# A hybrid decoder block on one core: product operands at the low end of SBUF, a new order for the first loads and casts, halved first units of the norms, and two users of ScalarE's tables swapped

## The chip, the cores and the metric

The kernel runs on one core of one Trainium2 chip, as one launch. The metric is the device time of that launch in microseconds. Weights and activations are float32 in HBM; the kernel streams some 503 MB of them through the core once.

## The reference

One decoder layer for 256 tokens of width 2048: a half-step SwiGLU feed-forward, a token mixer with eight dilated-attention heads and eight retention heads in parallel, a second half-step feed-forward, and a final RMSNorm. Each sub-layer reads a normed and modulated input; shifts, scales and gates come from one conditioning vector `c`.

```python
ada = (silu(c) @ w_ada + b_ada).reshape(9, D)          # shift, scale, gate, three times
h = rmsnorm(x, g_ffn1) * (1 + sc1) + sh1
x = x + 0.5 * gt1 * ((silu(h @ w1_gate) * (h @ w1_up)) @ w1_down)     # 2048 -> 5632 -> 2048
h = rmsnorm(x, g_mix) * (1 + sc2) + sh2
proj = h @ w_in                                        # 2048 -> 6144, split into q, k, v of both kinds and a gate
y = concat(dilated_attention(aq, ak, av), retention(rq, rk, rv) * silu(rg))
x = x + gt2 * (y @ w_out)                              # 2048 -> 2048
h = rmsnorm(x, g_ffn2) * (1 + sc3) + sh3
x = x + 0.5 * gt3 * ((silu(h @ w2_gate) * (h @ w2_up)) @ w2_down)
out = rmsnorm(x, g_final)
```

## The kernel before

Every large product is done in three passes of the reduced format fp32r. A factor is split into a rounded part and the rest ("hi" and "lo"), and `product_chunk` adds hi·hi, hi·lo and lo·hi in one PSUM bank. The activations are the stationary operand (128x128, loaded by LDWEIGHTS) and the weights the moving one (128x512).

- **Chunks.** All weights lie in HBM as 656 chunks of 128x1024 float32 (512 KB), in the order in which they are used. A chunk goes through a ring of four slots: SyncE loads it into `w_raw`, ScalarE writes its rounded part into `w_hi` (`w_hi`, L613), VectorE the rest into `w_lo` (`w_lo`, L808), and TensorE takes it with 12 matmuls (2 tiles of the contraction, 2 halves of the tokens, 3 passes; L1069, L1070, L1071). At the two inner norms, two chunks more are prepared in `w_hi_ahead` and `w_lo_ahead`.
- **Stationary operands.** There are three: `x_split` (the normed input, hi and lo), `hidden` (silu(gate) times up, hi and lo) and `projections_split` (the mixer's output, hi and lo). `hidden`, `projections`, `ada_early` and `x_turned` share one region of 48 KB per partition.
- **Groups.** A `Group` is the run of chunks that fills two PSUM banks. Feed-forward groups are GATE, UP and DOWN, those of the mixer IN and OUT. Their order is written out by `plan()`. GATE, UP and IN read `x_split`; DOWN reads `hidden`; OUT reads `projections_split`.
- **Order of the rest.** `schedule()` puts every other stage behind a chunk number: TensorE does its part of a stage after that chunk, and ScalarE and VectorE do theirs between the casts of the chunks. Each engine walks the table in its own program, and semaphores join them.
- **The opening.** `opening()` is the order of the first 68 chunks, in which the columns of `w_ada` are multiplied on VectorE too (`ada_tile`, L820, 1 MB each, four buffers `ada_early`). `x` is normed by ScalarE in quarters of 512 columns (`normed_first`, L671), turned by TensorE (`turn_x`, L1112, all eight ahead of the first product in TensorE's program), copied out of PSUM (`keep_x`, L676), and modulated slice by slice as soon as its columns of `w_ada` are done (`modulate_first`, L685 and L689; `low_first`, L932). Slice i of `x_split` is waited for by `operand`.
- **The inner norms** (`boundary(n, res)`). The last four chunks of a DOWN or OUT group are done for one half of the tokens and then for the other (`tail`). While the second half is multiplied, the first is normed. A norm is cut into eight units of 128 tokens by 512 columns (`UNITS`): `normed` (L926), `turn_unit` (L1123), `modulate` (L698), `split_x` (L941, L942). `head` does the first four chunks of the next group for one half and then the other, with the turning of later units between them.
- **The heads.** Square roots (`std`, L734) and SiLU (`silu_g`, L739) need different activation tables on ScalarE; a load of a table is an instruction of its own. `gated` (L1022), `turn_y` (L1201) and `split_ret` (L743, L1027) bring the retention output, in four pairs p of heads, into `projections_split`.

The lines that place the shared region and the ahead tiles are these:

```python
top = (nc.sbuf_usable_end - HID_BYTES) // 512 * 512
late_at = top - LATE * D * 4
hid = nc.alloc_sbuf_tensor_at("hidden", [P, FA * NT, 2 * T], F32R, offset=top)
proj_r = nc.alloc_sbuf_tensor_at("projections_split", [P, MIX_IN // P, T], F32R, offset=top)
```

In the built program this gives the following byte addresses within a partition (first byte to the byte behind the last), before and in the changed kernel:

```
tile                          before               changed
x_split (stationary)           32896 to  65664      65664 to  98432
w_hi (moving)                  82048 to  98432      98432 to 114816
w_lo (moving)                  98432 to 114816     114816 to 131200
scratch0 to scratch3          114816 to 131200     163968 to 180352
table (with the identity)     131200 to 145032     180352 to 194184
w_hi_ahead, w_lo_ahead        163328 to 179712     212480 to 228864
hidden, projections_split     179712 to 228864      16512 to  65664
residual, w_raw                16512 and 65664     131200 and 147584
```

Of the kernel before, what the change touches and what calls it, by code (L numbers as in the profile page):

```python
# [6 lines left out]
F32 = mybir.dt.float32  # L7
# [6 lines left out]
P = 128  # L14
# [90 lines left out]
UNITS = ((0, 0), (0, 1), (1, 0), (1, 1), (0, 2), (1, 2), (0, 3), (1, 3))  # L105
# [27 lines left out]
def schedule():  # L133
# [6 lines left out]
    def boundary(n, res):  # L140
# [7 lines left out]
        def units(name, *numbers):  # L148
            return [(name, 8 * n + u) for u in numbers]

        if n == 3:
# [6 lines left out]
        put(c0 + 4, *units("split_x", 2, 3), *units("xn", 4, 5, 6, 7), *units("mod", 4, 5))  # L158
        put(c0 + 5, *units("split_x", 4, 5), *units("mod", 6))
        put(c0 + 6, *units("split_x", 6), *units("mod", 7))  # L160
        put(c0 + 7, *units("split_x", 7))
# [54 lines left out]
    put(RET_FROM + 17, ("silu_g", 0), ("std", 1))  # L216
# [35 lines left out]
def opening():  # L252

    order = [("ada", i) for i in range(4)] + [("scale", 0), ("w", 0), ("low", 0)]
# [56 lines left out]
def build(nc, x_in, c_in, w_ada, b_ada, gains_in, g_final, w_all, table_in_hbm, out_t):  # L311
    with ExitStack() as ctx:  # L312
# [39 lines left out]
        HID_BYTES = FA * NT * 2 * T * 4  # L352
        assert HID_BYTES == (MIX_IN // P) * T * 4 == EARLY * D * 4 + DT * T * 4
        top = (nc.sbuf_usable_end - HID_BYTES) // 512 * 512
        late_at = top - LATE * D * 4
# [4 lines left out]
        hid = nc.alloc_sbuf_tensor_at("hidden", [P, FA * NT, 2 * T], F32R, offset=top)  # L360
        proj = nc.alloc_sbuf_tensor_at("projections", [P, MIX_IN // P, T], F32, offset=top)
        proj_r = nc.alloc_sbuf_tensor_at("projections_split", [P, MIX_IN // P, T], F32R, offset=top)
        ada_early = nc.alloc_sbuf_tensor_at("ada_early", [P, EARLY, D], F32, offset=top)
# [999 lines left out]
```

## Time and profile before

| | |
|---|---|
| median of 3 runs | 1925.22 us (1924.96 to 1925.38) |
| the profiled execution | 1925.92 us, its span 1924.1 us |
| TensorE matmul busy | 1882.3 us, 98% of the span |
| TensorE weight load busy | 1545.5 us, 80% |
| VectorE busy | 1310.5 us, 68% |
| ScalarE busy | 850.9 us, 44% |
| HBM read | 503.10 MB, 263 GB/s over the span |

The span runs from the first to the last instruction that the profiler saw. The 1.8 us between it and the time of the execution lie around the program. Busy shares are averages over stages with different limits.

### The profile page before, as it was taken

Reading aid. Unit: us, or ns where it says so; the run is one execution under the profiler, and the core shown is the slowest. Engines: PE = TensorE matmul, PEld = TensorE weight load, DVE = VectorE, ACT = ScalarE, POOL = GpSimd, SP = SyncE. Lnnn points to the kernel's source line nnn. Section 1 sums busy time; section 2 is a strip of 40 time slices with the busy share of each in tenths; the row PEclk is TensorE's granted clock in tenths of the full one; section 3 lists DMA queues with packets and bytes.
Section 4 is the critical chain, followed back from the end, with each engine's and each line's share of the span. In section 5 each row is a group of like instructions: output and inputs, shape, how many; then the busy total and the mean of one; then the engine's idle time right before and its main releaser. Section 6 shows DMA issues by size and latency. Waiting matters only on the chain. (4 is left out here: it accounts for less than half of the span.)

```text
span 1924.1 us, 21150 instructions
## 1 busy us (share of the span) xinstructions
PE 1882.3 (98%) x8392; PEld 1545.5 (80%) x8392; DVE 1310.5 (68%) x1350; ACT 850.9 (44%) x969; POOL 0.2 (0%) x4
## 2 busy tenths in 40 slices
PE   5899999999999999999999999999999999999998
PEld 4688888888888888788887787888888888888886
DVE  7798987887878878776665677666655454444454
ACT  5444444334444444645543546444443334444443
POOL 0000000000000000000000000000000000000000
PEclk7899999999999999999999999999999999999999
DMA  9898899888888887696454565777765556556563
GB/s 391 346 403 343 323 366 357 339 324 342 345 334 335 331 330 292 217 337 243 154 165 143 185 243 172 285 281 280 258 210 185 191 182 200 188 191 209 188 191 133
DMA packets 117889, 506.61 MB, mean 263 GB/s; under 512 B 13728, under 2 KB 13984, under 8 KB 98464
## 3 DMA queue, kind: packets, MB, share of 16 engines
q1 hardware_dynamic: 117792, 505.27, 72.0%
q8 instruction: 66, 1.08, 0.2%
q14 instruction: 31, 0.25, 0.0%
HBM read 503.10 MB, written 2.12 MB: 263 GB/s over the span
## 5 line engine op out<-in xcount | busy, mean ns | idle before, releaser
L808 DVE TENSOR_TENSOR w_lo<-w_raw,w_hi 128x1024 fp32r<-128x1024 f32 x652 | 795.1, 1223 | 516.0 <-ACT w_hi L613 515.4
L613 ACT CAST w_hi<-w_raw 128x1024 fp32r<-128x1024 f32 x652 | 684.1, 1051 | 1005.4 <-PE banks L1071 957.4
L1069 PE MATMUL banks<-w_hi,x_split 128*128 128x512 f32 x1776 | 703.2, 396 | 16.2 <-DVE x_split L932 16.2
L1071 PE MATMUL banks<-w_hi,x_split 128*128 128x512 f32 x1776 | 695.3, 391 | 0.0
L1070 PE MATMUL banks<-w_lo,x_split 128*128 128x512 f32 x1776 | 694.4, 391 | 0.0
L1069 PEld LDWEIGHTS banks<-w_hi,x_split 128*128 128x128 f32 x1776 | 335.7, 189 | 86.0 <-issue 13.2
L1071 PEld LDWEIGHTS banks<-w_hi,x_split 128*128 128x128 f32 x1776 | 335.2, 189 | 71.3
L1070 PEld LDWEIGHTS banks<-w_lo,x_split 128*128 128x128 f32 x1776 | 335.8, 189 | 68.1
L1069 PE MATMUL banks<-w_hi,hidden 128*128 128x512 f32 x704 | 278.2, 395 | 0.0
L1071 PE MATMUL banks<-w_hi,hidden 128*128 128x512 f32 x704 | 277.8, 395 | 0.0
L1070 PE MATMUL banks<-w_lo,hidden 128*128 128x512 f32 x704 | 277.7, 395 | 0.0
L820 DVE CUSTOM_DVE_ANT_0 scratch<-ada_raw,cond_row,ada 128x2048 bf16<-128x2048 f32 x112 | 262.7, 2345 | 0.1
L1071 PEld LDWEIGHTS banks<-w_hi,hidden 128*128 128x128 f32 x704 | 132.6, 188 | 30.9
L1070 PEld LDWEIGHTS banks<-w_lo,hidden 128*128 128x128 f32 x704 | 132.7, 188 | 30.8
L1069 PEld LDWEIGHTS banks<-w_hi,hidden 128*128 128x128 f32 x704 | 132.6, 188 | 30.7
L820 DVE CUSTOM_DVE_ANT_0 scratch<-ada_early,cond_row,ada 128x2048 bf16<-128x2048 f32 x32 | 75.1, 2347 | 1.4 <-DVE ada L820 0.6
L1069 PE MATMUL banks<-w_hi,projections_split 128*128 128x512 f32 x128 | 50.8, 397 | 0.0
L1071 PE MATMUL banks<-w_hi,projections_split 128*128 128x512 f32 x128 | 50.5, 395 | 0.0
L1070 PE MATMUL banks<-w_lo,projections_split 128*128 128x512 f32 x128 | 50.5, 394 | 0.0
L1071 PEld LDWEIGHTS banks<-w_hi,projections_split 128*128 128x128 f32 x128 | 24.1, 188 | 5.6
L1069 PEld LDWEIGHTS banks<-w_hi,projections_split 128*128 128x128 f32 x128 | 24.1, 188 | 5.5
L1070 PEld LDWEIGHTS banks<-w_lo,projections_split 128*128 128x128 f32 x128 | 24.1, 189 | 5.5
(133 smaller groups left out, 603.5 us busy)
## 6 DMA issues: line engine op xcount, KB each, us to landing
w_raw<-w_chunks SPq DMA_DIRECT2D x656, 512.0 KB, 4.2
ada_raw<-w_ada_tiles SPq DMA_DIRECT2D x112, 1024.0 KB, 6.0
ada_early<-w_ada_tiles SPq DMA_DIRECT2D x32, 1024.0 KB, 9.3
gate_row<-gate_rows SPq DMA_DIRECT2D x3, 1024.0 KB, 7.0
residual<-x_t SPq DMA_DIRECT2D x2, 1024.0 KB, 5.9
out_t<-residual SPq DMA_DIRECT2D x4, 512.0 KB, 3.1
table<-tables SPq DMA_DIRECT2D x1, 1664.0 KB, 9.7
cond_row<-g_final_t SPq DMA_DIRECT2D x1, 1024.0 KB, 5.4
```

Source lines behind the costliest of these rows:

```text
L613: nc.scalar.copy(w_parts(c)[0], raw[:, c % RING, :]).then_inc(hi_ready, 1)
L808: nc.vector.tensor_tensor(lo, raw[:, c % RING, :], hi.bitcast(F32), ALU.subtract).then_inc(lo_ready, 1)
L820: nc.vector.tensor_tensor_reduce(junk, src, c_row[:, :], 1.0, ada[:, m:m + 1], ALU.mult, ALU.add, ada[:, m:m + 1]).then_inc(ada_step, 1)
L1069: nc.tensor.matmul(o, x_hi, hi, start=(first and k == k0), stop=False, skip_group_check=True)
L1070: nc.tensor.matmul(o, x_hi, lo, start=False, stop=False, skip_group_check=True)
L1071: ins = nc.tensor.matmul(o, x_lo, hi, start=False, stop=(last and k == k0 + KC - 1), skip_group_check=True)
```

## The change

Four things change.

1. **Addresses.** The shared region (`hidden`, `projections_split` and what shares it) goes from the top of SBUF to the bottom, under the new name `stationary`; `x_split`, `w_hi` and `w_lo` follow it, and `residual` and `w_raw` come behind them. The ahead tiles go to the very top. No instruction of a product changes but for its addresses.
2. **The opening.** The first tile of `w_ada` is loaded ahead of `x`, the second between the halves of `x`. Both sums of squares are taken by ScalarE (the one on VectorE goes), and each engine copies one half of `cond_row` out of PSUM. VectorE does two tiles of `w_ada` before the reciprocal of the root. ScalarE does the cast of chunk 0 and the first modulation before the third quarter of `normed_first`, and the casts of chunks 1 and 2 move among the rest.
3. **Units of the norms.** The first two quarters of each half are cut in a unit of 2+2 tiles and one of 4; a norm has ten units now.
4. **The heads.** `std` 1 comes ahead of `silu_g` 0; `turn_y` and `split_ret` of pairs 2 and 3 come one chunk later.

```diff
-UNITS = ((0, 0), (0, 1), (1, 0), (1, 1), (0, 2), (1, 2), (0, 3), (1, 3))
+QUARTERS = ((0, 0), (0, 1), (1, 0), (1, 1), (0, 2), (1, 2), (0, 3), (1, 3))
+UNITS = ((0, 0, 2), (0, 2, 2), (0, 4, 4), (1, 0, 2), (1, 2, 2), (1, 4, 4), (0, 8, 4), (1, 8, 4), (0, 12, 4), (1, 12, 4))
...
-        put(c0 + 2, sums[0][0], sums[0][3], *units("xn", 0, 1), *units("mod", 0, 1))
-        put(c0 + 3, *units("split_x", 0), sums[1][0], *units("split_x", 1), *sums[1][1:], *units("xn", 2, 3),
-            *units("mod", 2, 3))
+        put(c0 + 2, sums[0][0], sums[0][3], *units("xn", 0, 1), *units("mod", 0, 1, 2))
+        put(c0 + 3, *units("split_x", 0, 1), sums[1][0], *units("split_x", 2), *sums[1][1:], *units("xn", 2, 3),
+            *units("mod", 3, 4, 5))
...
-    put(RET_FROM + 17, ("silu_g", 0), ("std", 1))
+    put(RET_FROM + 17, ("std", 1), ("silu_g", 0))
...
-        put(RET_FROM + 25 + p - 1, ("turn_y", p))
-        put(RET_FROM + 25 + p - 1, ("split_ret", p))
+        put(RET_FROM + 25 + p, ("turn_y", p))
+        put(RET_FROM + 25 + p, ("split_ret", p))
...
-    order = [("ada", i) for i in range(4)] + [("scale", 0), ("w", 0), ("low", 0)]
+    order = [("ada", 0), ("ada", 1), ("inverse", 0), ("ada", 2), ("ada", 3), ("scale", 0), ("w", 0), ("low", 0)]
...
-        xs = sb("residual", [P, 2, D])
+        low = (nc.sbuf_base + 31) // 32 * 32
+        sb("stationary", [P, HID_BYTES // 4])
         xsp = sb("x_split", [P, DT, 2 * T], F32R)
-        raw = sb("w_raw", [P, RING, CH])
         whi = sb("w_hi", [P, RING, CH], F32R)
         wlo = sb("w_lo", [P, RING, CH], F32R)
+        xs = sb("residual", [P, 2, D])
+        raw = sb("w_raw", [P, RING, CH])
...
-        top = (nc.sbuf_usable_end - HID_BYTES) // 512 * 512
-        late_at = top - LATE * D * 4
+        late_at = (nc.sbuf_usable_end - LATE * D * 4) // 512 * 512
...
-        hid = nc.alloc_sbuf_tensor_at("hidden", [P, FA * NT, 2 * T], F32R, offset=top)
+        hid = nc.alloc_sbuf_tensor_at("hidden", [P, FA * NT, 2 * T], F32R, offset=low)
...
+        def unit_count(m):
+
+            return SLICES + NU * (m[0] - 1) + m[1] + 1
...
+        def last_before(n, u):
+
+            quarter = QUARTERS.index((UNITS[u][0], UNITS[u][1] // 4)) - 2
+            if quarter < 0:
+                return SLICES + NU * (n - 1)
+            return SLICES + NU * (n - 1) + max(i for i, (t, k, _) in enumerate(UNITS) if QUARTERS.index((t, k // 4)) == quarter) + 1
...
             sp.dma_start(tab[:, 0:EARLY_COLS], table_in_hbm[:, 0:EARLY_COLS]).then_inc(ident_in, 16)
-            sp.dma_start(xs[:, 0, :], x_in[:, 0, :]).then_inc(x_in_sem[0], 16)
+            early_tile(0)
             sp.dma_start(ada[:, :], b_ada).then_inc(const_in, 16)
             sp.dma_start(gain[:, :, :], gains_in).then_inc(const_in, 16)
+            sp.dma_start(xs[:, 0, :], x_in[:, 0, :]).then_inc(x_in_sem[0], 16)
+            early_tile(1)
             sp.dma_start(xs[:, 1, :], x_in[:, 1, :]).then_inc(x_in_sem[1], 16)
-            for i in range(EARLY):
+            for i in range(2, EARLY):
                 early_tile(i)
...
             keep_x(0)
             keep_x(1)
+            w_hi(0)
+            modulate_first(0)
             normed_first(2)
             keep_x(2)
             keep_x(3)
+            w_hi(1)
             normed_first(3)
-            w_hi(0)
-            modulate_first(0)
             keep_x(4)
             keep_x(5)
-            w_hi(1)
+            w_hi(2)
             keep_x(6)
             keep_x(7)
-            w_hi(2)
             w_hi(3)
...
                     for i in range(TAIL):
                         if t == 0:
                             pe.wait_ge(lo_ready, g.first + i + 1)
-                            if i >= 2:
-                                turn_unit(8 * n + i)
+                            if i == 2:
+                                turn_unit(n, 3)
+                                turn_unit(n, 4)
+                            elif i == 3:
+                                turn_unit(n, 5)
```

**ScalarE in the opening, before.** The rows from the first root on; `scratch<-residual` is `normed_first`, `x_turned<-banks` is `keep_x`, `w_hi<-w_raw` a cast of a chunk.

```order
L671 ACTIVATE scratch<-residual,inverse_root 128x512 x4
L676 COPY x_turned<-banks 128x512 x2
L671 ACTIVATE scratch<-residual,inverse_root 128x512 x2
L676 COPY x_turned<-banks 128x512 x2
L671 ACTIVATE scratch<-residual,inverse_root 128x512 x2
L613 CAST w_hi<-w_raw 128x1024
L685 ACTIVATE scratch<-x_turned,ada,mod_scale 128x256 x2
L689 CAST x_split<-scratch 128x2x256
L676 COPY x_turned<-banks 128x512 x2
L613 CAST w_hi<-w_raw 128x1024
```

The same place in the changed kernel:

```order
L693 ACTIVATE scratch<-residual,inverse_root 128x512 x4
L698 COPY x_turned<-banks 128x512 x2
L635 CAST w_hi<-w_raw 128x1024
L707 ACTIVATE scratch<-x_turned,ada,mod_scale 128x256 x2
L711 CAST x_split<-scratch 128x2x256
L693 ACTIVATE scratch<-residual,inverse_root 128x512 x2
L698 COPY x_turned<-banks 128x512 x2
L635 CAST w_hi<-w_raw 128x1024
L693 ACTIVATE scratch<-residual,inverse_root 128x512 x2
L698 COPY x_turned<-banks 128x512 x2
L635 CAST w_hi<-w_raw 128x1024
```

The cast of chunk 0 and the first modulation moved ahead of the last two quarters of `normed_first`; behind the modulation, the cast of chunk 1 now has a quarter and two copies ahead of it where it had two copies.

**VectorE at the first inner norm, before.** From the split of the first unit on; `banks,gate_row` and `residual<-residual,scratch` are the residual of the second half of the tokens.

```order
L941 CAST x_split<-scratch 128x4x128
L942 TENSOR_TENSOR x_split<-scratch,x_split 128x4x128
L885 TENSOR_TENSOR scratch<-banks,gate_row 128x512
L891 TENSOR_TENSOR residual<-residual,scratch 128x512
L941 CAST x_split<-scratch 128x4x128
L942 TENSOR_TENSOR x_split<-scratch,x_split 128x4x128
L901 RECIPROCAL inverse_root<-root 128x1
```

The same place in the changed kernel:

```order
L965 CAST x_split<-scratch 128x2x128
L966 TENSOR_TENSOR x_split<-scratch,x_split 128x2x128
L965 CAST x_split<-scratch 128x2x128
L966 TENSOR_TENSOR x_split<-scratch,x_split 128x2x128
L908 TENSOR_TENSOR scratch<-banks,gate_row 128x512
L914 TENSOR_TENSOR residual<-residual,scratch 128x512
L965 CAST x_split<-scratch 128x4x128
L966 TENSOR_TENSOR x_split<-scratch,x_split 128x4x128
L924 RECIPROCAL inverse_root<-root 128x1
```

The first split is done in two halves; the residual of the second half of the tokens still stands between it and the next quarter's split.

**ScalarE in the heads, before.** `projections<-projections` is `silu_g`, `var<-var` is `std`, `projections_split<-banks` is `split_ret`.

```order
L739 ACT_TABLE_LOAD
L739 ACTIVATE projections<-projections 128x1024
L734 ACT_TABLE_LOAD
L734 ACTIVATE var<-var 128x8
L613 CAST w_hi<-w_raw 128x1024 x3
L743 CAST projections_split<-banks 128x512
L613 CAST w_hi<-w_raw 128x1024
L743 CAST projections_split<-banks 128x512
L613 CAST w_hi<-w_raw 128x1024 x3
L638 COPY projections<-banks 128x4x128 x2
L613 CAST w_hi<-w_raw 128x1024
L739 ACT_TABLE_LOAD
```

The same place in the changed kernel, up to the second `silu_g`:

```order
L757 ACTIVATE var<-var 128x8
L762 ACT_TABLE_LOAD
L762 ACTIVATE projections<-projections 128x1024
L635 CAST w_hi<-w_raw 128x1024 x3
L766 CAST projections_split<-banks 128x512
L635 CAST w_hi<-w_raw 128x1024
L766 CAST projections_split<-banks 128x512
L635 CAST w_hi<-w_raw 128x1024 x3
L660 COPY projections<-banks 128x4x128 x2
L635 CAST w_hi<-w_raw 128x1024
L762 ACTIVATE projections<-projections 128x1024
L635 CAST w_hi<-w_raw 128x1024 x2
```

Two of the three table loads are gone, the one ahead of the second `silu_g` among them, and one more cast of a chunk stands between that `silu_g` and the next `split_ret`.

## Rows read from the trace of the kernel before

**Rows 1.** The page, busy time, share of the span and instructions of TensorE.

```profile
PE 1882.3 (98%) x8392; PEld 1545.5 (80%) x8392; DVE 1310.5 (68%) x1350; ACT 850.9 (44%) x969; POOL 0.2 (0%) x4
```

**Rows 2.** Waits of TensorE: who waited for whom, us, times, longest.

```profile
PE banks L1069 <- DVE x_split L932: 16.2, 4, 5.1
PE banks L1112 <- ACT scratch L671: 8.4, 3, 6.9
PE banks L1069 <- DVE x_split L942: 2.2, 2, 1.1
PE banks L1201 <- DVE projections L1022: 1.6, 1, 1.6
PE banks L1123 <- DVE scratch L926: 1.2, 4, 0.5
```

**Rows 3.** Windows, TensorE alone: stretch, busy (count), clock, DMA.

```profile
100.00:200.00 100.00, 100.00 (x443) 1.00 0.94 368
340.00:440.00 100.00, 100.00 (x432) 1.00 0.87 335
1110.00:1160.00 50.00, 50.00 (x217) 1.00 0.65 230
```

**Rows 4.** The page's groups: one pass of each stationary operand.

```profile
L1069 PE MATMUL banks<-w_hi,x_split 128*128 128x512 f32 x1776 | 703.2, 396 | 16.2 <-DVE x_split L932 16.2
...
L1069 PE MATMUL banks<-w_hi,hidden 128*128 128x512 f32 x704 | 278.2, 395 | 0.0
...
L1069 PE MATMUL banks<-w_hi,projections_split 128*128 128x512 f32 x128 | 50.8, 397 | 0.0
```

**Rows 5.** Timeline, first norm: first and last of ten steps on ahead tiles.

```profile
783.19 0.39 PE L1070 MATMUL banks<-w_lo_ahead,x_split 128*128 128x512 f32 x1
...
785.51 0.40 PE L1071 MATMUL banks<-w_hi_ahead,x_split 128*128 128x512 f32 x1
```

**Rows 6.** Timeline of the opening: start us, us, instruction, idle before.

```profile
16.63 1.33 ACT L671 ACTIVATE scratch<-residual,inverse_root 128x512 f32<-128x512 f32 x2
20.21 1.09 PE L1112 MATMUL banks<-table,scratch 128*128 128x128 f32 x8 [1.10 <-ACT scratch L671]
24.51 1.06 ACT L676 COPY x_turned<-banks 128x512 f32<-128x512 f32 x2
25.47 1.06 ACT L613 CAST w_hi<-w_raw 128x1024 fp32r<-128x1024 f32 x1
25.48 0.77 PE L1069 MATMUL banks<-w_hi,x_split 128*128 128x512 f32 x1 [4.18 <-DVE x_split L932]
26.56 1.23 DVE L808 TENSOR_TENSOR w_lo<-w_raw,w_hi 128x1024 fp32r<-128x1024 f32 x1 [1.22 <-ACT w_hi L613]
38.79 0.39 PE L1071 MATMUL banks<-w_hi,x_split 128*128 128x512 f32 x1
44.31 0.77 PE L1069 MATMUL banks<-w_hi,x_split 128*128 128x512 f32 x1 [5.13 <-DVE x_split L932]
76.00 0.69 DVE L932 TENSOR_TENSOR x_split<-scratch,x_split 128x512 fp32r<-128x512 f32 x1 [0.72 <-ACT x_split L689]
```

**Rows 7.** Timeline of the first inner norm.

```profile
780.05 2.90 ACT L698 ACTIVATE scratch<-banks,ada,mod_scale 128x128 f32<-128x128 f32 x8 [1.17 <-issue]
782.80 1.09 ACT L613 CAST w_hi<-w_raw 128x1024 fp32r<-128x1024 f32 x1
782.88 0.47 PE L1069 MATMUL banks<-w_hi_ahead,x_split 128*128 128x512 f32 x1 [1.09 <-DVE x_split L942]
784.10 0.64 ACT L654 ACTIVATE scratch<-residual 128x512 f32<-128x512 f32 x1 [0.21 <-DVE residual L891]
```

**Rows 8.** Timeline of the heads, around the third `turn_y`.

```profile
1087.63 1.28 ACT L739 ACT_TABLE_LOAD   x1
1088.92 1.06 ACT L739 ACTIVATE projections<-projections 128x1024 f32<-128x1024 f32 x1
...
1090.83 0.66 PE L1201 MATMUL banks<-table,projections 128*128 128x128 f32 x4 [1.56 <-DVE projections L1022]
```

More of the change, by code:

```diff
@@ L148, in units @@
         def units(name, *numbers):
-            return [(name, 8 * n + u) for u in numbers]
+            return [(name, (n, u)) for u in numbers]
         if n == 3:
@@ L691, in modulate @@
             def modulate(m):
-                n, t, q, u = unit(m)
+                n, u = m
+                t, k0, tiles = UNITS[u]
                 act.wait_ge(scl_ready, SLICES + n)
-                act.wait_ge(xt_done, m + 1)
-                act.wait_ge(mod_ready, m - 1)
-                for i in range(4):
-                    k = 4 * q + i
-                    ins = nc.scalar.activation(plain(u)[:, i * P:i * P + P], ps[:, 4 + u % 4, i * P:i * P + P], ACT.Identity,
+                act.wait_ge(xt_done, unit_count((n, max(i for i, (half, k, _) in enumerate(UNITS) if (half, k // 4) == (t, k0 // 4)))))
+                act.wait_ge(mod_ready, last_before(n, u))
+                for i in range(tiles):
+                    k = k0 + i
+                    ins = nc.scalar.activation(plain_unit(u)[:, i * P:i * P + P], turned(u)[:, i * P:i * P + P], ACT.Identity,
                                                scale=scl[:, k:k + 1], bias=ada[:, 3 * n * DT + k:3 * n * DT + k + 1])
@@ L922, in normed @@
             def normed(m):
-                n, t, q, u = unit(m)
+                n, (t, q) = m[0], QUARTERS[m[1]]
                 if q >= 2:
-                    dve.wait_ge(xt_done, 8 * n + UNITS.index((t, q - 2)) + 1)
+                    last = max(u for u, (half, k, _) in enumerate(UNITS) if half == t and k // 4 == q - 2)
+                    dve.wait_ge(xt_done, unit_count((n, last)))
                 nc.vector.tensor_scalar(xn_buf(t, q), xs[:, t, GW * q:GW * q + GW], rinv[:, t:t + 1], None,
@@ L1114, in turn_x, with turn_unit @@
                 ins.then_inc(xt_done, 1)
-            def turn_unit(m):
-                n, t, q, u = unit(m)
-                pe.wait_ge(xn_ready, xn_count(m))
-                if u >= 4:
-                    pe.wait_ge(mod_f32, m - 3)
-                x = xn_buf(t, q)
-                for i in range(4):
-                    ins = nc.tensor.transpose(ps[:, 4 + u % 4, i * P:i * P + P], x[:, i * P:i * P + P], ident)
+            def turn_unit(n, u):
+                t, k, tiles = UNITS[u]
+                quarter = QUARTERS.index((t, k // 4))
+                pe.wait_ge(xn_ready, xn_count(n, t, k // 4))
+                if quarter >= 4:
+                    pe.wait_ge(mod_f32, SLICES + NU * (n - 1) + FREED[quarter])
+                x = xn_buf(t, k // 4)
+                for i in range(tiles):
+                    at = (k % 4 + i) * P
+                    ins = nc.tensor.transpose(turned(u)[:, i * P:i * P + P], x[:, at:at + P], ident)
                 ins.then_inc(xt_done, 1)
@@ L1245, in tail @@
                         if t == 1 and i == g.count - 1 and n < 3:
-                            turn_unit(8 * n)
-                            turn_unit(8 * n + 1)
+                            for u in range(3):
+                                turn_unit(n, u)
                         ins = product_chunk(g.first + i, halves(hid) if g.kind == DOWN else mixed, KC * i, 2 * g.side, False,
@@ L1289, in _ @@
                     if start and i % 2 == 0:
-                        pe.wait_ge(mod_ready, 8 * norm + min(i + 2, 8))
+                        pe.wait_ge(mod_ready, unit_count((norm, 7 if i == TAIL else NU - 1)))
                     chunk(g, i)
```

87 lines of the change are left out of this document (47 added, 40 removed).

## The prediction

> **What bounds the kernel now.** I read the page first: TensorE is busy for 98% of the span [rows 1], so only what lets a matmul follow the last one sooner, or takes a gap of TensorE away, can shorten the kernel. Then the waits of TensorE. They add up to some 30 us [rows 2], nearly all in the first 80 us: 16.2 us in four waits for a slice of `x_split`, 8.4 us for the normed `x`. Behind the opening TensorE waits twice for the first unit of an inner norm (2.2 us), four times for a later unit (1.2 us), and once in the heads, for `gated` (1.6 us). Everything else is matmul after matmul.
>
> So the question becomes what one matmul costs, and the busy time doesn't tell it: matmuls overlap, and their mean duration is 395 to 397 ns for all three stationary operands [rows 4]. What counts is the step from start to start. The windows give it. A matmul of 0.39 us is counted if it touches the window, so the step is (window + 0.39) / count. Between 100 and 200 us all products read `x_split`: 100.39 / 443 = 226.6 ns. Between 340 and 440 us all read `hidden`: 100.39 / 432 = 232.4 ns. Between 1110 and 1160 us all read `projections_split`: 50.39 / 217 = 232.2 ns [rows 3]. The granted clock is 1.00 in all three (the 2.4 GHz level), and the instructions have the same form. TensorE had no wait in the two slower stretches, and VectorE, ScalarE and the DMA engines are no busier there (DMA 0.94, 0.87, 0.65). What differs is where the stationary operand lies: 32,896 to 65,664 in the first, 179,712 and up in the other two.
>
> A second row speaks for the address and against the tile: at the first inner norm `x_split`, at its low place, is multiplied by the ahead tiles at 163,328 to 179,712. Ten steps take 785.51 - 783.19 = 2.32 us, 232 ns each [rows 5]. Either operand at a high address costs the same some 5.7 ns. Within the low region I see no slope: the 226.6 ns is a mean over `x_split` from 32,896 to 65,664 and over weights from 82,048 to 114,816. So it looks like a line between 114,816 and 163,328.
>
> **The addresses.** `hidden` is read by 3 x 704 matmuls and `projections_split` by 3 x 128 [rows 4], 2496 together. Each goes from 232.35 to 226.65 ns: 2496 x 5.7 = 14.2 us off. All of it lies on TensorE, which nothing else covers, so it comes off the end. The ahead tiles stay high; their 48 matmuls gain nothing. The cost side: `w_lo` now lies at 114,816 to 131,200, where no product operand has lain, and `x_split` as the stationary operand at 65,664 to 98,432, where so far only moving operands lay. The bounds are 0 (as all rows below 114,816) and 5.7 ns for each of the 3 x 1776 = 5328 matmuls of `x_split`, 30.4 us. I take 0: the new places are nearer to the region that is fast than to the nearest one known slow (163,328). The turning of tiles reads the identity and the scratch tiles, which go higher; eight turnings take 1.09 us [rows 6], and as the identity lies above 131,200 before as after, I take 0 there too.
>
> At this point a page speaks against the change. The Trainium skill, "TensorE: Matmul & The Clock Gate", section "Wait — 56ns, not 53.3ns?", gives start to start as the columns over the clock and some 2.5 ns, about 216 ns for 512 columns, and knows no address in it. By that rule the first term would be nothing. The trace differs from it in both stretches, with 226.6 and 232.4 ns.
>
> **The opening.** TensorE turns all of `x` before its first product. Before, the last eight turnings started at 20.21 and the first product at 25.48, when slice 0 was split [rows 6]. That split keeps its time: it needs the same 2 MB of `x` and 4 MB of `w_ada` to arrive, whatever their order. But now two quarters of `normed_first` stand behind it. From the end of the first modulation, 24.5: a quarter 1.33, two copies 1.06, a cast 1.06, a quarter 1.33, less some 0.1 of overlap at each, ends near 28.9; eight turnings of 1.09 us bring the first product to 30.1, 4.6 us later. This is covered: the first four chunks ended at 39.0 (last matmul at 38.79 [rows 6]) and TensorE then waited 5.1 us for slice 1, until 44.31. They end at 43.6 now. What is late instead is VectorE. Its `w_lo` of chunk 1 had waited 1.22 us for the cast at 25.47 and started at 26.56; the cast has a quarter more ahead of it, so it starts near 27.8, 1.2 us later. Behind it stand in one queue the tiles of `w_ada` and rests of chunks up to the split of slice 3 at 76.00 [rows 6], with next to no idle time, and TensorE waits for each slice at 44.31 and twice more. From there it never waits until the first norm. So +1.2 us reach the end. Bounds: 0, if the small gaps of VectorE absorb it, and +3, if the late first product holds back casts (they wait for its chunks) or TensorE's clock rises later after its last gap. The new order of the loads costs and gives nothing: the same bytes stand ahead of the fourth tile of `w_ada`, and the earlier first two `ada_tile` end in a wait for it.
>
> **The norms.** The first unit's modulation of eight tiles starts at 780.05 and takes 2.90 us, 0.36 a tile [rows 7]. With two tiles to wait for and a half-size split (half of 1.15 us and a fixed part, 0.75), the first half unit is ready at 780.05 + 0.75 + 0.75 = 781.6, just as TensorE ends the tail. The first wait, 1.1 us before 782.88, nearly goes. But `head` puts the turning of the second half's units ahead of its third chunk, and these come from the residual of the second half, whose sum of squares started at 784.10, behind ScalarE's cast that ended at 783.89 [rows 7]. That cast stays, so the second half is ready 0.15 us sooner at most. TensorE runs two chunks 1.1 us sooner and waits 1.1 us longer there. I take 0.15 us off at each of two norms, 0.3 in all; bounds 2.2 off (both waits really gone) and 0.6 on (extra fixed costs on VectorE).
>
> **The heads.** `turn_y` of pair 2 waited for `gated`, that for the SiLU at 1088.92, and that for the table load of 1.28 us at 1087.63 [rows 8]. The load goes, since nothing between the two SiLUs asks for another table, and TensorE comes a chunk (2.8 us) later. The last matmul ahead started at 1088.87 (1090.83 less the wait and a step), so the gap of 1.7 us beyond a normal step closes. OUT needs pairs 2 and 3 at its seventh and eighth chunk, three chunks after the turning, against some 2 us of ScalarE and VectorE work. `std` ahead of `silu_g` 0 puts 0.2 us on the first `gated`, which TensorE doesn't wait for. I take 1.7 off, bounds 1.3 and 1.9.
>
> **The sum.** -14.2 - 1.7 - 0.3 + 1.2 = -15.0 us. The profiled execution took 1925.92 us, 0.7 above the median of the runs, so it goes to 1910.9 and the median of 1925.22 to **1910.2 us**. Its own bounds: 1906 (opening 0, norms 2.2, heads 1.9) to 1913 (opening 3, norms 0.6 on, heads 1.3: 1925.2 - 11.9).
>
> **The rivals.** A change of 0.2% (3.9 us) is about what this measurement can tell from none.
>
> - **The line lies lower (slower).** If it is crossed by the new `w_lo` or, for stationary operands, by the new `x_split`, the 5328 matmuls of `x_split` slow down. With `hidden` still gaining, 1910.2 + 30.4 = 1940.6 us; if `w_lo` slows all three passes, also of `hidden`, 14.2 more, 1954.8. It decides as soon as half of the 5328 are hit (15.2 us). For it: nothing in the trace has been read at these places in a product, and `x_split` ended at 65,664. Against: no slope up to 114,816. Chance 0.08.
> - **Part of `w_lo` is over the line.** One slot of four, 656 matmuls of one pass and up to three times that, 3.7 to 11.2 us given back: 1914 to 1920 us. An opening worse than its bound looks the same. Chance 0.07.
> - **`w_lo` alone is slow.** A third of all 7824 matmuls at 232.4: 1910.2 + 2608 x 0.0057 = 1925.1 us. Chance 0.03.
> - **The address is not the cause.** Then the first term is nothing, and 1925.2 - 0.8 = 1924.4 us. For it: three stretches are few, and the stages differ in more than the address. Against: the ahead tiles with `x_split`, and two tiles of different layout with one step. Chance 0.07. By the page's rule this is what would happen. A variant, that the cause is the start address modulo 512 bytes (0 for the slow tiles, 128 for the fast ones), gives the forecast's time, as the moved tiles get 128.
> - **The forecast.** Chance 0.75.
>
> **Numbers.** The forecast and the second rival hold 0.82, so the range is 1906 to 1920. Faster 0.82, same 0.10 (the third and fourth rival), slower 0.08.
>
> **What the changed kernel's profile would show.** Windows over DOWN and OUT stretches with the same count as over `x_split` (443 in 100 us; 432 would be the layout failing, and fewer than 443 over `x_split` the line crossed). The first product at 30 us, the first wait for slice 1 of 2 instead of 5.1 us, the split of slice 3 at 77.2. At the norms no wait for the first unit, but some 1.3 us at the turning of the fourth; in the heads two table loads fewer and no wait of `turn_y`. I would be wrong above all if the step depended on what the weight loads and moving reads do to one another, and not on where each lies.

## The result, and the profile after

The changed kernel takes **1909.01 us** (1908.77 to 1909.29 in four runs), the kernel before 1925.09 us in the same comparison: ratio 0.9916, 95% interval 0.9904 to 0.9927. The forecast was 1910.2 us. The profiled execution took 1909.02 us, its span 1907.2 us.

Busy time on the page, and the waits of TensorE (us, times, longest), as in [rows 1] and [rows 2]:

```profile
PE 1865.6 (98%) x8392; PEld 1542.6 (81%) x8392; DVE 1310.6 (69%) x1357; ACT 849.6 (45%) x969; POOL 0.2 (0%) x4
```

```profile
PE banks L1136 <- ACT scratch L693: 16.4, 3, 12.2
PE banks L1093 <- DVE x_split L956: 10.6, 3, 4.9
...
PE banks L1149 <- DVE scratch L950: 2.8, 4, 0.9
```

The number of matmuls is the same and TensorE is busy 16.7 us less (1882.3 before). Its waits have moved: more for the normed `x` (16.4 against 8.4 us), less for the slices of `x_split` (10.6 against 16.2), none for the first unit of a norm and none at `turn_y` (L1227 now). The windows, to be read against [rows 3], and the page's groups, against [rows 4]:

```profile
100.00:200.00 100.00, 100.00 (x443) 1.00 0.94 367
340.00:440.00 100.00, 100.00 (x443) 1.00 0.90 341
1110.00:1160.00 50.00, 50.00 (x222) 1.00 0.68 234
```

```profile
L1093 PE MATMUL banks<-w_hi,x_split 128*128 128x512 f32 x1776 | 701.8, 395 | 10.6 <-DVE x_split L956 10.6
...
L1093 PE MATMUL banks<-w_hi,hidden 128*128 128x512 f32 x704 | 274.3, 390 | 0.0
...
L1093 PE MATMUL banks<-w_hi,projections_split 128*128 128x512 f32 x128 | 50.1, 391 | 0.0
```

Between 340 and 440 us 443 matmuls of `hidden` fit where 432 did. That is 100.39 / 443 = 226.6 ns from one start to the next (the step), as over `x_split`. OUT goes from 217 to 222 in 50 us.

The opening, to be read against [rows 6]:

```profile
24.23 1.33 ACT L693 ACTIVATE scratch<-residual,inverse_root 128x512 f32<-128x512 f32 x2
...
27.36 1.34 ACT L693 ACTIVATE scratch<-residual,inverse_root 128x512 f32<-128x512 f32 x2
27.50 1.23 DVE L831 TENSOR_TENSOR w_lo<-w_raw,w_hi 128x1024 fp32r<-128x1024 f32 x1 [2.45 <-ACT w_hi L635]
...
30.37 0.78 PE L1093 MATMUL banks<-w_hi,x_split 128*128 128x512 f32 x1
45.25 0.47 PE L1093 MATMUL banks<-w_hi,x_split 128*128 128x512 f32 x1 [2.24 <-DVE x_split L956]
76.51 0.69 DVE L956 TENSOR_TENSOR x_split<-scratch,x_split 128x512 fp32r<-128x512 f32 x1 [0.72 <-ACT x_split L711]
77.35 0.47 PE L1093 MATMUL banks<-w_hi,x_split 128*128 128x512 f32 x1 [3.48 <-DVE x_split L956]
```

The first product comes 4.9 us later (30.37 for 25.48), the `w_lo` of chunk 1 at 27.50 for 26.56, and slice 1 at 45.25 for 44.31. The first norm, against [rows 7], and the last SiLU of the heads, against [rows 8]:

```profile
773.83 2.90 ACT L721 ACTIVATE scratch<-banks,ada,mod_scale 128x128 f32<-128x128 f32 x8 [1.07 <-issue]
774.67 0.29 DVE L965 CAST x_split<-scratch 128x256 fp32r<-128x256 f32 x1 [0.60 <-ACT scratch L721]
...
775.57 0.47 PE L1093 MATMUL banks<-w_hi_ahead,x_split 128*128 128x512 f32 x1
...
779.54 0.63 PE L1149 MATMUL banks<-table,scratch 128*128 128x128 f32 x4 [0.95 <-DVE scratch L950]
```

```profile
1080.73 1.06 ACT L762 ACTIVATE projections<-projections 128x1024 f32<-128x1024 f32 x1
...
1084.97 0.60 PE L1227 MATMUL banks<-table,projections 128*128 128x128 f32 x4
```

At the norm the first product follows the tail without a wait, and a wait of 0.95 us stands at the turning of the fourth and fifth units. In the heads the second SiLU has no table load ahead of it (two loads instead of four in this stage), and `turn_y` follows at once.

I compared the starts of the 8392 TensorE instructions of the two executions, one by one. The changed kernel is 0.27 us ahead when the first product with `hidden` starts (312.08 for 312.35), and 16.9 us ahead at the last matmul (1898.52 for 1915.42). In between lie 2496 matmuls of `hidden` and `projections_split` (5.7 ns each, 14.2 us), two norms (0.3 us each) and the heads (1.7): 16.5 of the 16.6 us. At the first norm the three steps that hold a wait took 1.489 + 0.563 + 0.848 us before and take 0.399 + 1.346 + 0.850 now.

### The profile page after: what moved, and what is told of

It reads as the page before. It is cut to its first block and busy times, and to the rows that moved or that the text cites. A ratio compares the mean times of both kernels' runs of the same rounds, so it can differ in the third digit from the quotient of the medians.

```text
span 1907.2 us, 21163 instructions
## 1 busy us (share of the span) xinstructions
PE 1865.6 (98%) x8392; PEld 1542.6 (81%) x8392; DVE 1310.6 (69%) x1357; ACT 849.6 (45%) x969; POOL 0.2 (0%) x4
## 5 line engine op out<-in xcount | busy, mean ns | idle before, releaser
L1093 PE MATMUL banks<-w_hi,x_split 128*128 128x512 f32 x1776 | 701.8, 395 | 10.6 <-DVE x_split L956 10.6
L1093 PE MATMUL banks<-w_hi,hidden 128*128 128x512 f32 x704 | 274.3, 390 | 0.0
L1095 PE MATMUL banks<-w_hi,hidden 128*128 128x512 f32 x704 | 273.9, 389 | 0.0
L721 ACT ACTIVATE scratch<-banks,ada,mod_scale 128x128 f32<-128x128 f32 x64 | 24.0, 469 | 9.5 <-issue 6.3
```

The costliest lines, as they stand in the source:

```text
L721: ins = nc.scalar.activation(plain_unit(u)[:, i * P:i * P + P], turned(u)[:, i * P:i * P + P], ACT.Identity, scale=scl[:, k:k + 1], bias=a ...
L1093: nc.tensor.matmul(o, x_hi, hi, start=(first and k == k0), stop=False, skip_group_check=True)
L1095: ins = nc.tensor.matmul(o, x_lo, hi, start=False, stop=(last and k == k0 + KC - 1), skip_group_check=True)
```

## The experiments

**1. The address by itself.** A kernel with nothing but blocks of 48 products; it computes nothing of the layer. The scanned tiles lie every 4096 bytes from 98,432 to 221,312, and the fixed ones at 32,896 and 82,048; all of these starts are 128 modulo 256.

```diff
+            for t in tiles:
+                run(low_stat, t)
+            for t in tiles:
+                run(t, low_mov)
+            run(even_stat, low_mov)
+            run(low_stat, even_mov)
+            run(even_stat, even_mov)
```

> A kernel that leaves out the whole decoder: it fills tiles of SBUF with one piece of w1_gate and then issues blocks of 48 matmuls of the product form (fp32r, 128x128 stationary, 128x512 moving) with no wait between them; its output is x with one part overwritten. One operand stays at a low place (stationary at 32,896, moving at 82,048) and the other goes through 31 places from 98,432 to 225,408 in steps of 4,096, first the moving one and then the stationary one; then come blocks with tiles that start at a multiple of 512 at low addresses (40,960 and 90,112), and one with both operands high. Theory A, a line in the address of either operand: the step from matmul to matmul is some 226.7 ns in blocks below a line between 131,200 and 163,328 and some 232.4 above it, in both scans; the low blocks at multiples of 512 stay at 226.7. Theory B, the start address modulo 512: every tile of the scan (all start at 128 modulo 512) has 226.7, also above 163,328, and the low blocks at multiples of 512 have 232.4. Theory C, the stage and not the address: all blocks have the same step.

Timeline of TensorE, start and duration of a block; the names are those of the moving and the stationary tile:

```profile
62.04 11.04 PE L64 MATMUL banks<-at_aa,low_stat 128*128 128x512 f32 x48
...
388.44 11.04 PE L64 MATMUL banks<-at_be,low_stat 128*128 128x512 f32 x48
...
410.20 11.04 PE L64 MATMUL banks<-low_mov,at_aa 128*128 128x512 f32 x48
...
736.60 11.04 PE L64 MATMUL banks<-low_mov,at_be 128*128 128x512 f32 x48
...
758.37 11.32 PE L64 MATMUL banks<-low_mov,even_stat 128*128 128x512 f32 x48
769.52 11.30 PE L64 MATMUL banks<-even_mov,low_stat 128*128 128x512 f32 x48
780.66 11.05 PE L64 MATMUL banks<-even_mov,even_stat 128*128 128x512 f32 x48
```

Every block of both scans takes 11.04 us, up to 221,312, in either role, and so does one with both operands high (at_bc and at_ay). My line in the address is refuted. But when the stationary tile lies at 40,960 (0 modulo 512) and the moving one at 82,048 (128 modulo 512), 48 products take 769.52 - 758.37 = 11.15 us, some 232 ns each; the other way round 11.14 us. With both at 0 (the moving one at 90,112) they take 791.55 - 780.66 = 10.89 us, some 227 ns. So the slow step is there at low places too, and either tile alone is fast in another pair. That points at how the two starts stand to one another, which the next scan tests.

**2. How they have to stand.** The same kernel with two fixed tiles; s is what is added to the stationary operand's start (32,768) and m to the moving one's (81,920).

```diff
+            for m in moving:
+                run(0, m)
+            for s in stationary:
+                run(s, 0)
+            for n in both:
+                run(n, n)
```

`moving` and `stationary` go up to 512 bytes in steps of 32, `both` takes nine places of the same range; a number in these lists is an element of 4 bytes.

> Not the reference's work: blocks of 48 products of 128x128 by 128x512 (fp32r) with nothing else on the chip. The stationary tile starts at 32,768 + s bytes and the moving one at 81,920 + m, both 0 modulo 512 when s = m = 0. In order: m = 0 to 512 in steps of 32 bytes with s = 0; s = 32 to 512 with m = 0; both shifted by the same 32 to 480 bytes; m = 4, 8 and 16; m = 640 to 2048. If only the distance of the two starts modulo some power of two counts, all equal shifts stay at 226.7 ns a product, m = 128 and s = 128 give 232.2 ns, m = 512 gives 226.7, and the scan shows from which step on and with which period the slower step comes. If instead a start that is 0 modulo 512 is good for both operands alike or bad for one of them, the equal shifts differ from one another. If the slower step of the probe before came from the two places (40,960 and 90,112) and not from their alignment, the whole scan is flat.

Windows cut at the starts of blocks: stretch, its length, busy (count; 48 and the one that reaches in), loads (count), clock, DMA. In this order m = 0, 128, 256, then s = 128 and s = 256, then both at 128:

```profile
33.12:44.00 10.88, 10.88 (x49) 9.01 (x48) 0.00 (x0) 0.00 (x0) 1.00 0.00 0
...
77.41:88.61 11.20, 11.20 (x49) 9.01 (x48) 0.00 (x0) 0.00 (x0) 1.00 0.01 1
122.24:133.12 10.88, 10.88 (x49) 9.01 (x48) 0.00 (x0) 0.00 (x0) 1.00 0.00 0
266.76:277.92 11.16, 11.16 (x49) 9.04 (x48) 0.00 (x0) 0.00 (x0) 1.00 0.00 0
311.31:322.20 10.89, 10.89 (x49) 9.01 (x48) 0.00 (x0) 0.00 (x0) 1.00 0.00 0
454.89:465.79 10.90, 10.90 (x49) 9.01 (x48) 0.00 (x0) 0.00 (x0) 1.00 0.00 0
```

The mean step from start to start within each block, in ns, from the starts of its 48 matmuls:

```
offset in bytes    0     32    64    96    128   160   192   224   256   384   512
moving alone     226.7 233.4 229.1 233.6 233.4 234.1 233.2 233.2 226.8 233.4 226.8
stationary alone 226.7 233.2 233.4 234.2 232.5 233.4 229.0 233.4 226.7 232.5 226.7
both             227.2 227.2 227.2 227.2 227.2   -   227.6   -   227.6 226.7   -
moving by 4, 8 and 16 bytes: 236.7, 231.6, 231.7; by 768, 1024, 1536, 2048: 227.0, 226.7, 227.0, 226.7
```

What counts is the distance of the two starts **modulo 256 bytes**. I call a pair with a distance of 0 aligned. Aligned pairs take 226.7 to 227.7 ns, whatever the starts are; all others take 229.0 to 236.7. The two scans confirm one another: m = 64 and s = 192 are the same distance (moving less stationary start, modulo 256) and take 229.1 and 229.0, m = 128 and s = 128 are the same and take 233.4 and 232.5. The same pair (m = 128) took 232.2 ns when it was repeated near the end, so differences of 1 ns mean nothing here. Why a distance of 64 costs only 2.4 ns stays open.

**3. The addresses in the kernel.** First the change of addresses alone, on the kernel before:

```diff
+        low = (nc.sbuf_base + 31) // 32 * 32
+        sb("stationary", [P, HID_BYTES // 4])
...
-        top = (nc.sbuf_usable_end - HID_BYTES) // 512 * 512
-        late_at = top - LATE * D * 4
+        late_at = (nc.sbuf_usable_end - LATE * D * 4) // 512 * 512
```

> The kernel before with the addresses of the changed one and nothing else. The address as the cause of the step: 14.2 us less than the kernel before (ratio 0.9926), and the windows over DOWN and OUT at 443 matmuls in 100 us. If the layout does nothing: within 0.5 us of the kernel before.

Then everything but it: the changed kernel with these same lines, and the order of the tiles, turned back.

> The changed kernel with the addresses of the kernel before. If the parts add up and the layout gives 14.2 us of the 16 measured: 1.8 to 2 us less than the kernel before. By the prediction's sum for these three parts (1.2 on, 0.3 and 1.7 off): 0.8 us less.

Measured: addresses alone 1911.62 us (ratio 0.9927, 0.9914 to 0.9941; -13.9), all but them 1924.49 us (0.9993, 0.9984 to 1.0001; -1.1). Both are differences from the kernel before as it ran beside them. The addresses are nearly the whole gain. Whether the *low* place or the *alignment* gives it, the next two runs tell. The first is the kernel before, with the shared region (and the ahead tiles below it) 128 bytes further up:

```diff
-        top = (nc.sbuf_usable_end - HID_BYTES) // 512 * 512
+        top = (nc.sbuf_usable_end - HID_BYTES) // 512 * 512 + 128
```

> The kernel before with the shared region of hidden and projections (and the ahead tiles below it) 128 bytes further up, at 179,840 and 163,456, and nothing else changed. Theory of the relative start: all product operands then start at 128 modulo 512, the 2496 matmuls of hidden and projections step 226.7 ns in place of 232.4, and the ahead products too: -14.2 -0.3 = -14.5 us, 1911.1 us, as good as the whole change of addresses (-13.9). Theory of my prediction, a line in the address between 114,816 and 163,328: the operands are still far above it, 0.0 us, 1925.5 us.

```profile
340.00:440.00 100.00, 100.00 (x443) 1.00 0.90 345
```

1911.42 us (1910.80 to 1912.62), ratio 0.9924 (0.9912 to 0.9937), 14.7 us less than the 1926.08 of the kernel before beside it. At the top of SBUF, 443 products of `hidden` fit in 100 us. The second goes the other way round. The region stays at the low end of SBUF, but 128 bytes out of step with the weights; the rest is the changed kernel, with the ahead tiles as in experiment 4:

```diff
-        low = (nc.sbuf_base + 31) // 32 * 32
-        sb("stationary", [P, HID_BYTES // 4])
+        low = (nc.sbuf_base + 31) // 32 * 32 + 128
+        sb("stationary", [P, HID_BYTES // 4 + 64])
```

> The kernel changed_ahead_128 (the changed kernel with the ahead tiles at 212,608) with the shared region at 16,640 in place of 16,512 and 128 bytes of padding behind it: at the low end as the change wants it, but 0 modulo 256, while x_split (65,920), w_hi (98,688) and w_lo (115,072) stay at 128 modulo 256. Theory of the relative start (the scan of offsets: 226.7 ns where the two starts agree modulo 256, 232.2 to 232.5 where they are 128 apart): the 2496 matmuls of hidden and projections go back to 232.4 ns, +14.2 us on 1909.4, 1923.6 us. Theory that the low place pays: 0.0, 1909.4 us.

```profile
340.00:440.00 100.00, 100.00 (x432) 1.00 0.88 334
```

1924.2 us (1923.55 to 1925.37), ratio 0.9994 (0.9984 to 1.0003): it is 14.8 us slower than the same kernel with the region in step (1909.4, experiment 4; 15.4 if each is taken against the kernel before beside it), and 432 in 100 us are back. The gain of the addresses is gone, at the same low place. So the place does nothing that these runs can tell, and the alignment gives the gain.

**4. The ahead tiles.** The changed kernel leaves them at 212,480, 0 modulo 256, out of step with `x_split`.

```diff
-        late_at = (nc.sbuf_usable_end - LATE * D * 4) // 512 * 512
+        late_at = (nc.sbuf_usable_end - LATE * D * 4 - 128) // 512 * 512 + 128
```

> The changed kernel with the ahead tiles at 212,096 or 212,608 (128 modulo 512) in place of 212,480 (0 modulo 512). Theory of the relative start: the ahead products step 226.7 ns in place of 232, about -0.3 us, 1908.7 us; that is less than the runs can tell in the median but shows in the steps of the trace at 780 us. Theory of the address line: the ahead tiles are above it as before, 0.0 us and steps of 232 ns.

1909.4 us (1909.12 to 1910.01) against 1909.01: no gain that can be told. The first 19 steps with an ahead tile at the first norm (those that hold a turning or a wait left out) went from a mean of 232.1 to 229.7 ns, not to 226.7. The trace of the changed kernel shows why I had misread the same place before. These are aligned products, of `x_split` with the ring, right behind the turning at 779.54:

```profile
780.24 0.39 PE L1094 MATMUL banks<-w_lo,x_split 128*128 128x512 f32 x1
...
781.17 0.39 PE L1095 MATMUL banks<-w_hi,x_split 128*128 128x512 f32 x1
```

Four steps in 0.93 us, 232 ns each: in this stretch aligned products are slow too. In the kernel before, the 12 aligned ring steps next behind [rows 5] have a mean of 231.7 ns, beside 231.9 for the ten steps of [rows 5] themselves; the same ten steps on aligned ahead tiles, in this experiment's trace, have 230.7.

This is not special to a norm. It follows the turnings, and here is one far from any norm, in the changed kernel:

```profile
536.94 1.04 PE L1128 MATMUL banks<-table,scratch 128*128 128x128 f32 x8
...
538.05 0.39 PE L1094 MATMUL banks<-w_lo,x_split 128*128 128x512 f32 x1
...
540.36 0.39 PE L1095 MATMUL banks<-w_hi,x_split 128*128 128x512 f32 x1
...
541.94 0.39 PE L1093 MATMUL banks<-w_hi,x_split 128*128 128x512 f32 x1
```

The ten steps from 538.05 to 540.36 take 2.31 us, 231 ns each; the next seven take 1.58 us, 226 ns each. In this trace, later than 100 us, 20 groups of small matmuls (18 of them turnings) are followed by at least 30 products of `x_split`. The second to tenth step behind them has a mean of 229.7 ns, and from the eleventh on every step is 226 or 227 ns. The work of ScalarE and VectorE for the norm, on the other hand, doesn't show: between 764.07 and 772.91, ahead of the first turning of the norm, 39 aligned steps take 8.84 us, 226.7 ns each, while both work on the residual, the squares and the root. So the slow steps come with the turnings (and behind a wait, as at [rows 5]). No run leaves the turnings out, so why they do it stays open.

**5. The parts.** Each of the other three alone on the kernel before:

```diff
-    put(RET_FROM + 17, ("silu_g", 0), ("std", 1))
+    put(RET_FROM + 17, ("std", 1), ("silu_g", 0))
...
-        put(RET_FROM + 25 + p - 1, ("turn_y", p))
+        put(RET_FROM + 25 + p, ("turn_y", p))
```

> The kernel before with std 1 ahead of silu_g 0 and turn_y and split_ret of pairs 2 and 3 one chunk later, nothing else. The wait of turn_y as the whole of it: 1.7 us less (1.3 to 1.9), no wait of turn_y in the trace. If the wait only goes to another place, as to the y_ready of OUT: within 0.5 us of the kernel before.

Measured 1923.91 us, ratio 0.9991 (0.9982 to 1.0), -1.6 us; two table loads are gone, and TensorE's list of waits has none for `gated` any more.

```diff
+UNITS = ((0, 0, 2), (0, 2, 2), (0, 4, 4), (1, 0, 2), (1, 2, 2), (1, 4, 4), (0, 8, 4), (1, 8, 4), (0, 12, 4), (1, 12, 4))
```

> The kernel before with the ten units of the norms and nothing else. Wait moved (the prediction): 0.2 to 0.5 us less, the wait for the first unit (1.1 us) gone and one of 0.9 to 1.3 us at the turning of the fourth unit. Wait gone: 2.2 us less.

Measured 1925.2 us against 1925.93, ratio 0.9995 (0.9986 to 1.0004), -0.7 us. The wait for the first unit is gone from the timeline and this one stands instead, as in the changed kernel:

```profile
785.59 0.63 PE L1147 MATMUL banks<-table,scratch 128*128 128x128 f32 x4 [0.95 <-DVE scratch L948]
```

The opening alone, its loads and orders:

```diff
-            for i in range(EARLY):
+            for i in range(2, EARLY):
                 early_tile(i)
...
+            w_hi(0)
+            modulate_first(0)
```

> The kernel before with the new opening and nothing else. By the prediction's sum: 1.2 us more than before, from VectorE's queue. By the trace of the changed kernel, where slices 1 to 3 are 0.9 to 1.0 us late but the clock is back at its high level sooner after the last gap (78 instead of 82 us): 0.3 us less, and more or less by 2 us with the moment at which the clock rises, which nothing in the program sets; then single runs of this kernel should spread by more than 1 us.

Measured 1926.53 us against 1925.93, ratio 1.0003 (0.9994 to 1.0012), +0.6 us: slices 1 and 2 restart at 45.91 and 61.97 (44.31 and 60.36 before). Heads, units and opening are each inside what these runs can tell from nothing, so the traces say more of them than the medians. In the medians the parts add up to -13.9 - 1.6 - 0.7 + 0.6 = -15.6 us; together they gave -16.1.

**6. Inside the opening.** First the changed kernel with the old order of ScalarE only:

```diff
-            w_hi(0)
-            modulate_first(0)
...
+            w_hi(0)
+            modulate_first(0)
```

> The changed kernel with ScalarE's order of the opening as before (the cast of chunk 0 and the first modulation behind all four quarters of normed_first, one more cast between the copies), its other parts kept. If the quarter ahead of the cast of chunk 1 is what makes VectorE's queue late: the first product comes at 25.5 to 27 instead of 30.4, slices 1 to 3 about 1 us sooner, and the kernel is 1 us faster than the changed one, if the clock rises at the same distance from the last gap. If the new loads are what counts: as the changed kernel.

```profile
26.64 1.10 ACT L707 ACTIVATE scratch<-x_turned,ada,mod_scale 128x256 f32<-128x256 f32 x2
...
48.10 0.77 PE L1093 MATMUL banks<-w_hi,x_split 128*128 128x512 f32 x1 [6.11 <-DVE x_split L956]
80.22 0.76 PE L1093 MATMUL banks<-w_hi,x_split 128*128 128x512 f32 x1 [4.94 <-DVE x_split L956]
```

1911.12 us (1910.92 to 1912.1), ratio 0.9923 (0.9911 to 0.9936). I had expected it 1 us faster than the changed kernel, and it is 2.1 us slower in the medians (1.3 us, if each is taken against the kernel before as it ran beside it; the intervals of the two ratios overlap). The trace says why. With the new loads the second half of `x` lands later: the first quarter is normed at 17.52 in the changed kernel (18.41 in this run), at 12.76 in the one before. In the old order the first modulation stands behind all four quarters (each of both halves of the tokens), and that brings it to 26.64, where the changed kernel has it at 22.58. The split of slice 0 and, by VectorE's queue, every slice behind it come some 3 us later. So the new order of ScalarE makes up for what the new loads cost.

Then the changed kernel without the opening's part, its loads and orders as before:

```diff
-            early_tile(0)
+            sp.dma_start(xs[:, 0, :], x_in[:, 0, :]).then_inc(x_in_sem[0], 16)
```

> The changed kernel with the loads and ScalarE's order of the opening left as before: addresses, units and heads alone. By the parts as timed alone (-13.9, -0.7 and -1.6 us) 16.2 us less than before, 1909.4 us; by the opening's own +0.6 it is 0.6 us faster than the changed kernel, so 1908.4 to 1909.4 us. Rival, from the profile of the changed kernel, where the half-speed stretch of the opening ended sooner and the stage of the hidden tiles began 0.27 us earlier than before: the opening's part pays 0.3 us once the others are there, 1909.3 to 1909.8 us. The two lie within what these runs can tell; first product and slices 1 to 3 in the trace (29.3, 44.3, 60.4 and 76.8 us expected) say more than the median.

```profile
25.60 0.76 PE L1092 MATMUL banks<-w_hi,x_split 128*128 128x512 f32 x1 [4.17 <-DVE x_split L955]
...
76.93 0.77 PE L1092 MATMUL banks<-w_hi,x_split 128*128 128x512 f32 x1 [5.33 <-DVE x_split L955]
```

1908.5 us (1906.88 to 1909.65), ratio 0.991 (0.9896 to 0.9924), the fastest kernel here by 0.5 us (0.85, if each is taken against the kernel before beside it), which its interval doesn't tell from the changed one. The starts agree in sign: slice 3 at 76.93 for 77.35, the last matmul at 1897.99 for 1898.52.

## Why the prediction was right in its number and wrong in its cause

**The bound and the step.** Right. TensorE waited for nothing in the two slower stretches, and the step from start to start was the quantity to read. 2496 x 5.7 ns = 14.2 us was forecast; -13.9 (addresses alone), -14.7 (the old place plus 128 bytes) and -14.8 (the difference of the two low versions, 1924.2 and 1909.4) were measured.

**The cause.** Wrong. The step that failed is "so it looks like a line between 114,816 and 163,328", and with it "either operand at a high address costs the same". The trace of before held five places, and in all five "high" and "out of step by 128 bytes" came together: 179,712 and 163,328 are 0 modulo 256, and 32,896, 82,048 and 98,432 are 128. The one variant that I had under the fourth rival (the start modulo 512) gave the same time and was the nearer one; what is true of neither operand alone is true of their distance, modulo 256. That is the case that the prediction's last sentence named as its main way of being wrong. The number was right by luck: the change happens to put every product operand at 128 modulo 256, but for the ahead tiles, and nobody chose these remainders. The same move to the low end with the region at 16,640 (experiment 3) is in full accord with my line in the address and gives 1924.2 us. The three rivals in which `w_lo` or `x_split` crosses the line had no object.

**The second witness.** [rows 5] was no evidence. Close behind a turning or a wait, aligned products take 231 to 232 ns as well (experiment 4), so those ten steps would have read nearly the same at any address. I should have read the ring's products beside them.

**The rule for one step.** The rule that I weighed, from the Trainium skill, "TensorE: Matmul & The Clock Gate", section "Wait — 56ns, not 53.3ns?", gives some 216 ns for 512 columns at any address. The traces disagreed before, and disagree in every aligned block with 226.7 ns; the 229 to 237 ns of the others it doesn't foresee. At 1.2 GHz the same section of the Trainium skill gives the columns over the clock and nothing more, 426.7 ns. There the traces agree: the half-speed steps behind slice 3 take 426 to 427 ns. The Trainium skill, "TensorE: Matmul & The Clock Gate", section "Step-by-step: what each phase is for", says that the two operands have read ports of their own, so that the next load takes no bandwidth from the running matmul. The scans limit that: with nothing but the start of one operand changed, 48 products took 10.88 or 11.20 us, so the two operands are not free of one another. Whether it is their reads that meet, no run here shows.

**The opening.** +1.2 was forecast. The steps came as foreseen: first product at 30.37 (30.1), `w_lo` of chunk 1 at 27.50 (27.8), the first wait for a slice 2.24 us instead of 5.13, slice 1 0.94 us late (1.2). Two sizes were off. VectorE's gaps absorbed a part: the split of slice 3 was at 76.51, 0.5 us late, not 1.2 (77.2). That holds beyond one execution: TensorE's first product with slice 3 starts at 77.24 us in the mean of the six traces with the old opening and at 77.70 in the five with the new one. And the clock came back sooner behind it. Before and after, windows of TensorE:

```profile
78.00:80.00 2.00, 2.00 (x7) 0.50 1.06 438
80.00:82.00 2.00, 2.00 (x6) 0.50 0.96 385
```

```profile
78.00:80.00 2.00, 2.00 (x7) 0.50 1.09 449
80.00:82.00 2.00, 2.00 (x8) 0.66 0.96 391
```

100 matmuls from slice 3's first took 25.20 us before and 24.40 after, as 11 steps of 426 to 427 ns became 7; so 0.51 us late became 0.29 early. That is luck of one execution rather than a gain. With the old opening the same 100 take 24.12 to 25.43 us in six traces (5 to 12 full steps at half speed), with the new one 24.14 to 25.52 in five (again 5 to 12); `all_but_opening`, with the old one, has the granted clock at 0.95 between 80 and 82 us and takes 24.30 us. The medians say +0.6 (alone) and +0.5 or +0.85 (with the rest, experiment 6). Neither is clear of nothing, but both fit the 0.5 us of slice 3.

**The norms and the heads.** Mechanisms and places as forecast: the first wait gone, one of 0.95 us at the turning of the second half instead. I had 0.3 us for two norms; 0.6 (steps) and 0.7 (median) were measured. Heads: -1.7 forecast, -1.6 measured. The total of 16.1 us off is larger than the 15.0 forecast by the opening's 0.6 to 1.5 and the norms' 0.3. One slip in the sum: its own lower bound (opening 0, norms 2.2, heads 1.9) comes to 1906.9 us and not to 1906.

## What to carry to other kernels

Give the stationary and the moving operand of a long run of fp32r products starts that agree modulo 256 bytes; here 128 bytes in one line of the allocation, put into the kernel before, gave 14.7 us, where the whole change to four parts gave 16.1. Read the step from start to start (window over count): the mean durations before (395 to 397 ns) didn't tell the slow stretches from the fast one. Read it away from turnings and waits. And when a slow and a fast group differ in where they lie, list every property of the address, size, place and remainder, before naming one: five places can agree in two properties at once, and only an experiment that parts them tells which one counts.

## What the runs showed of the hardware

- A 128x128 by 128x512 fp32r product steps 226.7 ns where both operands start at the same place modulo 256 bytes, and 229.0 to 236.7 ns where they don't, at the full granted clock. The worst was a distance of 4 bytes, 236.7 ns.
- With the starts agreeing modulo 256, the place in SBUF has no effect on either operand from 98,432 to 221,312: 62 blocks of 48 products, 11.04 us each.
- Behind turnings and other small matmuls on TensorE, aligned products step 229.7 ns in the mean of the second to tenth step (20 places of the changed kernel), and 226 or 227 ns from the eleventh on. Why was not tried.
- The half-speed stretch behind the last gap of the opening differs between executions of the same opening: 5 to 12 full steps of 426 to 427 ns with either opening (eleven traces), which makes the first 100 matmuls behind the gap take 24.12 to 25.52 us.
